# Skip term inside the causal kernel, shifted state writes, two tables in flight, per-tile GELU split, and a norm interleaved with the last down projection

## The reference, cut to what matters

```python
xp = xp + swiglu(rmsnorm(xp, norm_ffn[0]), ...)      # end of layer 0
hp = rmsnorm(xp, norm_mix[1])                        # the norm called k=2 below
# s5_mixer(h, ...): 64 groups of 16 channels, 64 complex states each
x_re, x_im = bb_re @ ug, bb_im @ ug                  # per group
s_re, s_im = scan of  s[t] = a * s[t-1] + x[t]       # complex, over time
y  = (c_re @ s_re - c_im @ s_im) + d_skip * u        # skip term d_skip * u
gl = gelu(y) @ w_glu
out = gl[:, :D] * sigmoid(gl[:, D:])
```

## Time and profile before

| | us |
|---|---|
| median of 3 runs (lowest, highest) | 2913.93 (2909.53, 2920.15) |
| the profiled execution, first to last instruction | 2920.8 |
| PE busy | 2608.9 (89%) |
| DVE busy | 1225.4 (42%) |
| POOL busy | 860.6 (29%) |
| ACT busy | 699.1 (24%) |
| granted clock of PE, mean | 0.920 |

### The profile page before, as it was taken

How to read it: one execution, slowest core, us unless ns; L and a number is a source line. 1 busy time by engine, 2 the same in 40 slices (tenths; PEclk the granted TensorE clock), 3 DMA queues, 4 the chain that set the end, 5 groups by cost and what they waited for, 6 DMA issues and landing times.

```text
span 2920.8 us, 38816 instructions
## 1 busy us (share of the span) xinstructions
PE 2608.9 (89%) x15202; PEld 2467.2 (84%) x15202; DVE 1225.4 (42%) x2116; ACT 699.1 (24%) x1143; POOL 860.6 (29%) x618
## 2 busy tenths in 40 slices
PE   6997837778888999999999868699889999999998
PEld 4997735556788999999999846599789999999998
DVE  3699748877132222222222567622412222222224
ACT  3321137666222111111111212321221111111114
POOL 2322223333344222222222400133442222222223
PEclk9998957767899999999999967699999999999999
DMA  4354452110301111111111257521011111111111
GB/s 106 136 167 163 159 153 50 42 38 1 126 22 44 44 43 43 43 43 45 50 49 43 92 159 211 166 68 49 17 44 44 48 49 47 43 43 43 43 43 62
DMA packets 226152, 210.30 MB, mean 72 GB/s; under 512 B 26832, under 2 KB 200832, under 8 KB 224656
## 3 DMA queue, kind: packets, MB, share of 16 engines
q1 hardware_dynamic: 219248, 177.86, 20.9%
q0 software_dynamic: 6816, 31.26, 2.9%
HBM read 151.94 MB, written 54.79 MB: 71 GB/s over the span
## 4 chain that ended last, share of the span: by engine, by line
PE 70%; DVE 8%; POOL 2%; ACT 2%; DMA 1%; issue 1%; SPq 1%; POOLq 0%; DVEq 0%; ACTq 0%
PE ps L229 21%; PE ps L231 21%; PE ps L230 21%; PE ps L1008 3%; PE ps L1390 2%; PE ps L1020 1%; PE ps L1388 1%; DVE fbuf L406 1%; DVE v L1452 1%; DVE tz L952 1%; DVE esp L963 1%; POOL hlo L414 1%; DVE qS L933 1%; PE ps L999 1%; SPq L1306 1%
## 5 line engine op out<-in xcount | busy, mean ns | idle before, releaser
L229 PE MATMUL ps<-hhi,whi 128*128 128x384 f32 (+1 forms) x3168 | 1047.2, 331 | 96.3 <-POOL wlo L223 37.2
L230 PE MATMUL ps<-hlo,whi 128*128 128x384 f32 (+1 forms) x3168 | 1042.3, 329 | 0.0
L231 PE MATMUL ps<-hhi,wlo 128*128 128x384 f32 (+1 forms) x3168 | 1042.0, 329 | 0.0
L229 PEld LDWEIGHTS ps<-hhi,whi 128*128 128x128 f32 x3168 | 602.5, 190 | 105.5 <-issue 39.5
L230 PEld LDWEIGHTS ps<-hlo,whi 128*128 128x128 f32 x3168 | 602.8, 190 | 0.2
L231 PEld LDWEIGHTS ps<-hhi,wlo 128*128 128x128 f32 x3168 | 602.5, 190 | 0.0
L223 POOL TENSOR_TENSOR wlo<-raw,whi 128x1024 fp32r<-128x1024 f32 x176 | 421.5, 2413 | 127.8 <-ACT whi L219 126.9
L554 DVE TENSOR_TENSOR fbuf<-ps,abuf 128x384 f32<-128x384 f32 x132 | 70.7, 535 | 906.2 <-ACT abuf L462 901.9
L495 POOL TENSOR_TENSOR gl<-fbuf,gh 128x384 f32 (+1 forms) x132 | 127.8, 968 | 980.7 <-DVE gh L557 980.7
L565 DVE TENSOR_TENSOR x<-ps,x 128x384 f32<-128x384 f32 (+1 forms) x528 | 282.6, 535 | 221.5 <-PE ps L231 220.3
L229 PE MATMUL ps<-gh,whi 128*128 (+2 forms) x1056 | 344.6, 326 | 0.0
(11 more groups left out here) (233 smaller groups left out, 2469.6 us busy)
## 6 DMA issues: line engine op xcount, KB each, us to landing
raw<-in_ffn_w_gate SPq DMA_DIRECT2D x44, 512.0 KB, 3.8
raw<-in_ffn_w_up SPq DMA_DIRECT2D x44, 512.0 KB, 3.8
raw<-in_ffn_w_down SPq DMA_DIRECT2D x44, 512.0 KB, 3.6
zT<-zst POOLq DMA_DIRECT2D x20, 544.0 KB, 4.9
raw<-in_ab_w_in SPq DMA_DIRECT2D x20, 512.0 KB, 5.3
x<-xs SPq DMA_DIRECT2D x2, 4352.0 KB, 13.8
raw<-in_ssm_w_glu SPq DMA_DIRECT2D x16, 512.0 KB, 3.9
dE<-eb POOLq DMA_DIRECT2D x4, 1632.0 KB, 6.7
```

The lines of the kernel that those rows point to most:

```text
L229: pe.matmul(out, wh, rh, start=first, stop=False)
L230: pe.matmul(out, wh, rl, start=False, stop=False)
L231: return pe.matmul(out, wl, rh, start=False, stop=last)
```

## The change

The mixer and the norm ahead of it are rewritten in five places.
- **Norm k=2.** DVE goes through the last down projection itself. In chunk c of 1 and 2, after its add m=2, it takes the reciprocal of chunk c-1, and after each of m=3 to 6 it writes two `hp` products of that chunk. PE's `sum_pe` of c-1 stands behind m=1 of chunk c, ACT's root behind the square of m=2. Chunk 2 is done behind the down as before.
- **Skip term.** Eight small DMAs fetch d_skip by channel (`dcol`), DVE builds diagonal blocks `dd` once, and `skip(f)` adds them to the first 16 columns of `kt`, on 16 partitions, before `tm` is spread. The copy to `kt` moves from DVE to ACT, between the copies of B and X, and waits for `t_made` of f-1. The add into `yp` goes.
- **States.** The last rotation steps write straight into `sh` (rows of 137, shifted by one); two copies and two memsets per tile go. `xx` is released when the third and fourth products have read it.
- **Tables and SP's order.** `e3` has two buffers, `u` is loaded two tiles ahead in SP's order, `p4` is loaded behind `u` and `e3` of tile 0. `dY` is now issued by POOL.
- **GELU and split by tile.** `yt` has one buffer. ACT's third(f) reads `zb`, applies GELU into `yt` and writes `hhi` of the tile; POOL (DVE for the last) writes `hlo`. GLU's first pair waits for tile k of the low part.

```diff
+        yt, oa = plan(off_a, ("yt", [P, T], F32))
...
+        def norm_steps(dve, c, tiles):
+            s, n = CHUNKS[c]
+            for f in tiles:
+                out = hp[:, f * T:(f + 1) * T].rearrange("p (s n) -> p n s", s=L)[:, s // L:(s + n) // L, :]
+                xf = x[:, f * T + s:f * T + s + n].rearrange("p (n s) -> p n s", s=L)
+                rf = rms[:, c % 2, 0:n].rearrange("p (n s) -> p n s", s=L)
+                dve.scalar_tensor_tensor(out, xf, cols[:, 8 + f:9 + f], rf, ALU.mult, ALU.mult).then_inc(sem("n_f"), 1)
...
+                    if f.l == 0 and c and m == 2:
+                        norm_root(act, 2, c - 1)
...
-                        if i is None and f.l == 0 and c == NC - 1 and m >= KD - 2:
-                            sum_pe(pe, f.norm + 1, m - (KD - 2))
+                        if i is None and f.l == 0 and c and m == 1:
+                            sum_pe(pe, 2, c - 1)
...
+            for c, (s, n) in enumerate(CHUNKS):
+                for m in range(KD):
+                    v = f.acc + (PARTS - 1) * KD * NC + c * KD + m
+                    dve.wait_ge(sem("acc_ready"), v + 1)
+                    xo = x[:, m * T + s:m * T + s + n]
+                    dve.tensor_tensor(xo, acc(v)[:, 0:n], xo, ALU.add).then_inc(sem("acc_used"), 1)
+                    if c and m == 2:
+                        norm_recip(dve, 2, c - 1)
+                    if c and 3 <= m < 7:
+                        norm_steps(dve, c - 1, range(2 * (m - 3), 2 * (m - 2)))
+            norm_recip(dve, 2, NC - 1)
+            norm_steps(dve, NC - 1, range(KD))
...
             def store_h(f):
                 sp.wait_ge(sem("n_f"), n_units(2, 2 * KD + f + 1))
-                sp.dma_start(dU[f * P:(f + 1) * P, :], hp[:, f * T:(f + 1) * T]).then_inc(sem(f"u_out{f % 2}"), 16)
...
-            def load(f):
+                sp.dma_start(dU[f * P:(f + 1) * P, :], hp[:, f * T:(f + 1) * T]).then_inc(sem(f"u_out{f % 4}"), 16)
+
+            def load_bc(f):
                 if f >= 1:
-                    sp.wait_ge(sem("e_BT"), 2 * f)
                     sp.wait_ge(sem("s_K"), f)
                 if f >= 3:
                     sp.wait_ge(sem("s_Y"), f - 2)
                 js = slice(4 * f, 4 * f + 4)
                 sp.dma_start(br[:], dB[:, js, :, :]).then_inc(sem("br_loaded"), 16)
                 sp.dma_start(ca[:, f % 3], dC[:, js, :, :]).then_inc(sem(f"ca_loaded{f % 2}"), 16)
+
+            def load_u(f):
                 if f >= 2:
                     sp.wait_ge(sem("s_Y"), f - 1)
-                if f == 0:
-                    store_h(0)
-                    store_h(1)
-
-                sp.wait_ge(sem(f"u_out{f % 2}"), 16 * (f // 2 + 1))
-                if f + 2 < NF:
-                    store_h(f + 2)
+                sp.wait_ge(sem(f"u_out{f % 4}"), 16 * (f // 4 + 1))
                 for s in range(L):
                     sp.dma_start(u[16 * s:16 * s + 16, f % 2, :, :],
                                  dU[f * P:(f + 1) * P, s * NCH:(s + 1) * NCH].rearrange("(g c) n -> c g n", c=16)
                                  ).then_inc(sem(f"u_loaded{f % 2}"), 16)
-                if f >= 1:
-                    sp.wait_ge(sem("s_rot"), f)
-                else:
-                    sp.wait_ge(sem("x_out"), 16 * (1 + NC))
-                    sp.wait_ge(sem("n_f"), n_units(2))
-                sp.dma_start(e3[:], dE[:, :, js, :]).then_inc(sem("e3_loaded"), 16)
...
-            load(0)
-            for f in range(NF + 1):
-                if f < NF:
-                    sp.wait_ge(sem("e_K"), 2 * f + 2)
-                    if f >= 2:
-                        sp.wait_ge(sem("s_Y"), f - 1)
-                    sp.wait_ge(sem("t_zero"), 1)
-                    for s in range(L):
-                        sp.dma_start(tm[16 * s:16 * s + 16, f % 2, :, 16 * s:P], kt[0:16, :, 0:P - 16 * s]).then_inc(sem(f"t_made{f % 2}"), 16)
-                if f + 1 < NF:
-                    load(f + 1)
-                if f:
-                    g = f - 1
-                    sp.wait_ge(sem("e_Y"), 4 * g + 4)
-                    if g >= 2:
-                        sp.wait_ge(sem(f"z_loaded{g % 2}"), 16 * (g // 2))
-                    for t in range(L):
-                        sp.dma_start(dY[g * P:(g + 1) * P, t * NCH:(t + 1) * NCH].rearrange("(g c) n -> c g n", c=16),
-                                     yy[16 * t:16 * t + 16, g % 2, :, :]).then_inc(sem(f"y_stored{g % 2}"), 16)
-            sp.wait_ge(sem("y_f"), NF)
+
+            def load_e(f):
+                if f >= 2:
+                    sp.wait_ge(sem("s_rot"), f - 1)
+                sp.dma_start(e3[f % 2][:], dE[:, :, 4 * f:4 * f + 4, :]).then_inc(sem(f"e3_loaded{f % 2}"), 16)
+
+            load_bc(0)
+            store_h(0)
+            store_h(1)
+            for g in range(8):
+                sp.dma_start(dcol[0:16, 8 * g:8 * g + 8], cols[16 * g:16 * g + 16, 40:48]).then_inc(sem("dcol_loaded"), 16)
+            load_u(0)
+            sp.wait_ge(sem("x_out"), 16 * (1 + NC))
+            sp.wait_ge(sem("n_f"), n_units(2))
+            load_e(0)
+            sp.wait_ge(sem("p_out"), 16)
+            sp.dma_start(p4[:], dP).then_inc(sem("p4_loaded"), 16)
+            store_h(2)
+            store_h(3)
+            load_bc(1)
+            sp.wait_ge(sem("w_lo"), SLAB_GLU + 2)
+            load_e(1)
+            load_u(1)
+            for f in range(NF):
+                sp.wait_ge(sem("e_D"), f + 1)
+                if f >= 2:
+                    sp.wait_ge(sem("s_Y"), f - 1)
+                sp.wait_ge(sem("t_zero"), 1)
+                for s in range(L):
+                    sp.dma_start(tm[16 * s:16 * s + 16, f % 2, :, 16 * s:P], kt[0:16, :, 0:P - 16 * s]).then_inc(sem(f"t_made{f % 2}"), 16)
+                if f + 4 < NF:
+                    store_h(f + 4)
+                if f + 2 < NF:
+                    load_bc(f + 2)
+                    load_u(f + 2)
+                    load_e(f + 2)
+            for p in range(2):
+                sp.wait_ge(sem(f"y_stored{p}"), 16 * L * (NF // 2))
+            sp.wait_ge(sem("y_g"), NF)
+            sp.wait_ge(sem("s_rot"), NF)
...
+                if f == 1:
+                    pe.wait_ge(sem("e_K"), 2)
...
+                act.wait_ge(sem("s_K"), f + 1)
+                if f:
+                    act.wait_ge(sem(f"t_made{(f - 1) % 2}"), 16 * L * ((f - 1) // 2 + 1))
+                for b in range(2):
+                    act.activation(kt[0:16].rearrange("p (j a) n -> p a j n", a=2)[:, b],
+                                   ps[0:16, 2 + b, :].rearrange("p (j n) -> p j n", j=4), ACT.Copy).then_inc(sem("e_K"), 1)
                 act.wait_ge(sem("s_X"), f + 1)
                 if f:
-                    act.wait_ge(sem("s_rot"), f)
+                    act.wait_ge(sem("s_xx"), f)
+                else:
+                    act.wait_ge(sem("x_out"), 16 * (1 + NC))
+                    act.wait_ge(sem("n_f"), n_units(2))
...
             def third(f):
-                act.wait_ge(sem("y_f"), f + 1)
-                yt = yp[:, f * T:(f + 1) * T]
-                act.activation(yt, yt, GELU).then_inc(sem("y_g"), 1)
-
-            for f in range(NF + 3):
+                act.wait_ge(sem(f"z_loaded{f % 2}"), 16 * (f // 2 + 1))
+                if f:
+                    act.wait_ge(sem("ys_lo"), f)
+                act.activation(yt[:].rearrange("p (n s) -> p n s", s=L), zb[f % 2][:].rearrange("p (s n) -> p n s", s=L), GELU
+                               ).then_inc(sem("y_g"), 1)
+                act.wait_ge(sem("y_g"), f + 1)
+                act.activation(hhi[:, f * T:(f + 1) * T], yt[:], ACT.Copy).then_inc(sem("ys_hi"), 1)
+
+            for f in range(NF + 2):
                 if f < NF:
                     first(f)
                 if 1 <= f <= NF:
                     second(f - 1)
-                if f >= 3:
-                    third(f - 3)
+                if f >= 2:
+                    third(f - 2)
+
+        def y_lo(eng, f, done):
+
+            eng.wait_ge(sem("ys_hi"), f + 1)
+            eng.tensor_tensor(hlo[:, f * T:(f + 1) * T], yt[:], hhi[:, f * T:(f + 1) * T].bitcast(F32), ALU.subtract
+                              ).then_inc(sem(done), 1)
 
         def s5_pool(pool):
             for f in range(NF):
+                pool.wait_ge(sem("e_Y"), 4 * f + 4)
+                for t in range(L):
+                    pool.dma_start(dY[f * P:(f + 1) * P, t * NCH:(t + 1) * NCH].rearrange("(g c) n -> c g n", c=16),
+                                   yy[16 * t:16 * t + 16, f % 2, :, :]).then_inc(sem(f"y_stored{f % 2}"), 16)
+                if f >= 2:
+                    y_lo(pool, f - 2, "ys_lo")
                 pool.wait_ge(sem(f"y_stored{f % 2}"), 16 * L * (f // 2 + 1))
-                if f >= 2:
-                    pool.wait_ge(sem("y_f"), f - 1)
                 pool.dma_start(zb[f % 2][:], dY[f * P:(f + 1) * P, :]).then_inc(sem(f"z_loaded{f % 2}"), 16)
+            y_lo(pool, NF - 2, "ys_lo")
...
```

(59 more changed lines are left out.)

112 lines of the change are left out of this document (48 added, 64 removed).

## The result

The change makes the kernel slower. Its median is 2990.64 us (2982.03 to 2994.59, 4 runs), against 2917.04 us for the kernel before, run beside it (2909.53 to 2927.48, 4 runs). The ratio is 1.0241, with a 95% interval from 1.0206 to 1.0276. The forecast was 2966, in a range from 2925 to 2992: the direction and the range hold, the range by no more than 1.4 us. The loss is 74 us by the two medians, 70 by the ratio, where 52 was forecast.

A forecast was written before the change was run, and what follows sets the result against it. The prediction took the mixer as the place, PE's Y and X starts being set by other engines' queues and slowed by the clock. Loop +54, front +2.4, tail -4.5 gave +52 on 2913.9: 2966 us, range 2925 to 2992.

The forecast's parts named there:

- part 1: SP's order in the mixer loop: each next Y has its table behind the end of Y(f), a 14.2 us gap.
- part 2: POOL and ACT in the loop: low part behind dY issues holds bt and X, a 16.2 us gap (15.6 to 21.0).
- The rival with issues at double: POOL's dY issues in the loop cost 1.2 us each, four gaps of 21.0: 2999 us, chance 0.12.
- part 3: Loop sum: slow Ys of 15.6 plus gaps, 219.4 against 156.3, less 9 for raised clocks: +54 us.
- The forecast's +63: Mixer loop by the skill page alone, no slow X raising the clock for the Y behind it: +63 us.
- part 4: DVE in the loop: tile falls to about 13 us, worth nothing with gaps of 14 and more.
- part 5: Norm in the last down: last hp 3.5 us later; with dcol, Y(0) 2.4 us later (-7 to +6).
- part 6: Tail behind the loop: first GLU chunk through at 20 instead of 26.5, net -4.5 us (-7 to 0).
- The rival on the other side: Mixer: PE never stands still long enough to lose its clock level; 2898 us (chance 0.06) or 2914 us (0.07).

The follow-up runs named there:

- the fastest version: Changed kernel with both reorderings, norm taken back, and SP's dcol, e3 and GLU slab loads moved ahead: 2898.54 us, 0.9926 to the kernel before.

## Why the prediction was right, and where its sizes were off

- **SP's order (part 1): right.** Forecast 14.2 us, measured 15.55 and 13.97. For Y(1) the terms are: `u` 4.9 (4.5), `e3` 0.7 (0.7), `tm` 5.1 (5.2), landing until `kt` 3.6 (2.3), `kt` and semaphores 1.2 (1.4). Short were the landing and, by 0.4, `u`. In front of Y(2) `u` took 3.7, `e3` 1.5, and the landing the 2.3 of the forecast. The run with the table ahead shows the place.
- **POOL's order (part 2): right, by two errors that cancel.** Forecast 16.2 (its terms add up to 16.1), measured 16.15 to 16.56. The eight `dY` issues took 4.18, not 4.8; GELU and the copy took 3.2, not 2.4, because GELU is strided in the kernel after, and I took its cost from the row of one that works in place. The rival with issues at double is refuted by the same row, 0.52 an issue.
- **Which Ys are slow (part 3): the term that was mis-sized.** I took one in three of the slow Xs to raise the clock, 9 us. All four did, so the Ys of the loop are 98.8 us in all and not 115.8: 17.0 less. The reason is visible in the two kinds of gap. Where PE waits ahead of X, X starts at the lower level and the level rises by its end or just behind it; where PE waits behind X, Y starts low and stays there. The row of 1760.51, from which "one in three" came, has the first kind of wait and a slow Y. Five traces have this kind of gap in front of Y(3) to Y(6) (the kernel after, and the runs with SP's order alone, the added matmuls, GELU's write and the norm taken back). Of their 20 Ys 14 took 8.8 to 9.4 and six 15.70. So the share to take was nearer seven in ten; that all four did so here is the luck of this execution, and the order doesn't fix it.
- **The price of fast Ys (part 3): missed.** Y(7) was to follow 1.4 behind Y(6), its scan of 13 us beside a Y of 15.6. Behind a Y of 8.76 it isn't covered: 8.89 us of waiting for `sh`, and then PE is at the lower level, 15.67. This gives back 7.5. The other gaps were 1.9 longer. With -17.0 the loop is 7.6 below the forecast of 210.4.
- **The Trainium skill** (TensorE: Matmul & The Clock Gate, section "HAM oscillation") has short bursts between waits for DMAs start at the half clock every time. The trace agrees for what stands right behind the wait: Y(1) and Y(2), and the X ahead of Y(3) to Y(6), 3.49 to 3.90 instead of 2.08 behind waits of 5.9 to 7.0. The X of 1698.23, which the forecast held against it, started slow as well. The forecast's +63 took the Y behind such an X to be slow too; that doesn't hold, 8.8 to 9.4, and the trace has 46.5.
- **DVE's savings worth nothing (part 4): right.** DVE is busy 29 us less in all, and the time is longer; `kt` on DVE waits 17.1 us at the longest. That they stay worth little once the gaps are gone was not forecast: I had put 3 us a tile on them. With both orders turned and the norm taken back the loop is 154.0, and 150.0 in the fastest version, so 2 to 6 below before and not 8 times 3 (PE's gaps are still 8 to 12 us there).
- **The norm (part 5): the mechanism was right, and the term of two `hp` beside the adds was mis-sized.** Forecast +3.5 for the last `hp` series, measured +9.6. Two `hp` beside the adds were priced at 1.49 from a series that ran with POOL idle. Between the adds of 384 columns a pair takes 2.42 and between those of 320 columns 2.23, and one round 2.74 and about 2.48 instead of 2.05 and 1.98. Over eight rounds this is some 4.8 of the missing 6.1. The rest is mostly in the chain that ends chunk 1, from DVE's second add of chunk 2 to the end of the second reciprocal: 8.2 where the forecast had 6.8, with PE's sum at 1.65 instead of 0.8. The chain of the last chunk is 0.5 longer, and the adds behind the rounds of chunk 1 are 0.5 shorter. What I did see, that PE, ACT, POOL and DVE then wait for one another, is what PE's waits of 5.11 and 10.18 for `ssum` show.
- **`dcol` (part 5):** eight issues in 5.82, above the 3.6 to 5 that I gave. The front loses 1.8 more than the norm explains (68.2 before, 70.0 with the norm taken back), close to the 1.2 that stand in the forecast.
- **The tail (part 6): wrong sign.** Forecast -4.5, measured +4.3. I followed tile 7 through POOL and SP, and that part is right: its low part on DVE ends 19.2 us behind the last Y, against 18. I didn't follow ACT's own queue behind it. There the first sigmoid stands behind the slab conversion, which stands behind SP's loads, which stand behind the reload of `x`. That the reload waits for the last GELU is in the forecast, at 15.4 after the last Y (measured 16.9, before 12.8), but not what stands behind it. `dY` on POOL landed a median of 2.8 us after its issue in the mixer, where SP's took 3.1 before, so it isn't the later for being on POOL. The run with two slabs earlier shows it, -9.
- **The sum.** In the trace 62.4 of the 66.0 us are in the edited stretches, against 52. The two large misses, the front (norm and `dcol`) with +9.2 and the tail with +8.8, were partly hidden by the loop, -7.6. That is luck: without it the time would have been near 2998, outside the range. The 3.1 before the edited part belong to the execution: in the 14 traces this mark lies between 1647.0 and 1653.2, and the kernel after has the latest.
- **The rival on the other side** (PE never stands still long enough) is refuted as a forecast of this kernel, with a wait of 6.06 in front of a slow Y. That both orders turned measure 155.9, between its 154 and 161.6, doesn't bear out its price: there the gaps are 8.3 to 11.7 us and not 12 to 14, two Ys are slow, and Y(7) waits 13.1.

What stays open: which of the slow Xs raise the clock and which don't. Rows with the same wait show both.

## What to carry to other kernels

When a change makes a load or a table deeper, write out the queue of the engine that issues it, and ask which wait the next tile's data now stand behind: the wrong order on SP and on POOL cost 46 us here. With both put right the change is 0.4% slower than before, and 0.7% faster only with the norm taken back and three more moves of that kind. Of two stalls one behind the other, removing one may gain nothing, as POOL's alone did here (SP's alone gained 29 us, both 57), since the matmuls that follow start at the lower clock as long as the other is there; try both together before either is dropped. And work moved between the instructions of a busy phase is to be priced beside its neighbours there, not by the rows of where it ran alone.
